# Two transformer blocks on one core: the norms of the second block keep the last chunk in PSUM, and the third unit starts inside the norm

## Chip, core and metric

The kernel runs on one core of a Trainium2 chip. The metric is the device time of one execution in microseconds (us); lower is better. The engines are named as in the profile: PE (TensorE matmul), PEld (its weight loads), DVE (VectorE), ACT (ScalarE), POOL (GpSimd) and SP (SyncE, which issues the loads).

## The reference, cut to what matters

`x` is 512 tokens by 1024 channels. The first block (attention, a state-space branch and a convolutional FFN) runs once and hands `x` on. The second block has two layers, and each layer has three sublayers, each with a norm ahead of it and one behind it:

```python
def _rmsnorm_2(x, g):
    x32 = x.astype(jnp.float32)
    y = x32 * lax.rsqrt(jnp.mean(x32 * x32, axis=-1, keepdims=True) + RMS_EPS)
    return (y * g.astype(jnp.float32)).astype(x.dtype)

def _swiglu(h, w_gate, w_up, w_down):
    return (jax.nn.silu(h @ w_gate) * (h @ w_up)) @ w_down

for l in range(2):
    f = _swiglu(_rmsnorm_2(x, g[0]), ffn_w_gate[l, 0], ffn_w_up[l, 0], ffn_w_down[l, 0])
    x = x + 0.5 * _rmsnorm_2(f, g[1])
    m = _mixer(_rmsnorm_2(x, g[2]), w_in[l], ...)
    x = x + _rmsnorm_2(m, g[3])
    f = _swiglu(_rmsnorm_2(x, g[4]), ffn_w_gate[l, 1], ffn_w_up[l, 1], ffn_w_down[l, 1])
    x = x + 0.5 * _rmsnorm_2(f, g[5])
```

The hidden width of these FFNs is 2816. Where one sublayer ends and the next begins, the kernel needs two token factors: 1/rms of `f` (call it inv_f), with which `x` is updated, and 1/rms of the new `x` (inv_u).

## The kernel before, in words

**Layout.** Channels lie on the 128 partitions, tokens on the free axis. `x`, `f` (output of a sublayer) and `u` (input of the next) are 8 chunks of 128x512. Every float32 product is made of three fp32r products: a weight is split into w_hi (ACT, L1232) and w_lo = raw - w_hi (POOL, L514), an input into u_hi and u_lo. A **unit** is one 128x512 output in a PSUM bank: for each of k chunks three products (lines 655 to 657), so 24 products for 8 chunks and 33 for the 11 chunks of half an FFN's hidden width. Units come in pairs p, slot s=0 into unit_bank0 and s=1 into unit_bank1, and the two weight slots are refilled in turn: SP loads, ACT rounds after the unit before is done, POOL subtracts.

**Order.** Each engine's program is written out by hand, with semaphores between them; there is no planner. An FFN of the second block is done in two halves of the hidden width: 11 pairs of gate and up units, then 4 pairs of down units (`down`, L848) that give the 8 chunks of `f`. After the first half DVE copies the chunks from PSUM into `f` (`f_out`, L2361); in the second half it adds the bank to `f` (`take_f`, L2294). After the mixer it copies them (`take_new`, L2298).

**The norm** (`norm(r)`, r = 1 to 5; r = 0 and r = 6 have code of their own, which the change leaves in essence alone). r = 1, 3, 4 follow an FFN and r = 2, 5 a mixer. While the last four pairs run, DVE and ACT keep running sums over the chunks: squares of f (ACT L1249, DVE L2256), squares of gain times f (ACT L1251, DVE L2231) and x times gain times f (DVE L2235, L2238). From these three sums the mean square of the new `x` follows before the new `x` is there. Then, once the last unit ends:

1. DVE takes the last chunk (L2300 or L2296), ACT squares it (L1249).
2. PE sums over the channels with products against a column of ones (`token_sums`, L710): f_acc at once, the last squares when they come. ACT takes the root (L1242), DVE the reciprocal (L2273), and PE spreads inv_f over a bank (`spread`, L725).
3. DVE meanwhile makes the cross product of the last chunk (L2235, L2238), ahead of the reciprocal, and the last sum of gf_sq (L2231), behind it. PE sums both (16 instructions L710), ACT copies the totals (L1308), and POOL works out the mean square of the new `x` (`grow_x`, L584).
4. DVE updates `x` chunk by chunk (L2351 into a unit bank, L2353), ACT makes u_hi (L1304) and, for six chunks, the unrounded u_all (L1310), POOL the u_lo of those six (L615), DVE the last two (L2285).
5. PE runs `first_units` (L729): the first two units of the next sublayer, side by side, chunk by chunk as `x` comes: four products with u_hi for chunk c (L748), then two with u_lo of chunk c-1 (`low`, L738). Their weights have buffers of their own, and they go into score0 and score1. After chunk 6 inv_u is spread.
6. Then comes the third unit, the first in unit_bank0 (L1200 in an FFN, L917 in the mixer): 24 products. Its bank is one of the two through which DVE updates `x`.

Between the sums PE issues products of the identity with itself, whose result nobody reads (`keep_warm`, L702): 3 after the first sums, 3 after the second, 4 after the last. In the trace each float32 product on PE (sums, spreads, identities) is two instructions.

The mixer's first scores (`z(0)`, L882 to L893) need q and k, which DVE takes after the first two units, turned by four DMAs that SP issues (`turn_heads`, L447 to L456).

## Time and profile before

| what | us |
|---|---|
| median of three runs | 2474.32 (2474.09 to 2474.41) |
| span of the profiled execution | 2472.5 |
| PE busy | 2459.4 (99% of the span) |
| PEld busy | 2010.1 (81%) |
| DVE busy | 1189.9 (48%) |
| POOL busy | 1070.6 (43%) |
| ACT busy | 912.5 (37%) |
| PE's share in the chain that ended last | 85%, with "issue" 9% |

The span runs from the first to the last instruction that the profiler saw, and the device time lies 1.8 us above it. PE's busy time is not PE's best: its matmuls are pipelined, so their recorded durations (390 ns for a 128x512 product) overlap, and the distance from start to start is what a product costs. The five norms r = 1 to 5 begin, with the first sum after the last unit, at 965.15, 1160.99, 1528.77, 1896.58 and 2092.46 us.

### The profile page before, as it was taken

What the parts mean: (1) busy time and instruction counts of PE and PEld (TensorE: products, weight loads), DVE (VectorE), ACT (ScalarE), POOL (GpSimd) and SP (SyncE); (2) the same over time, 40 slices, a digit from 0 to 9 for tenths busy, and PEclk for the clock granted to TensorE, in tenths of its full rate; (3) what the DMA queues carried; (4) which work ended last, traced back from release to release, by engine and by line L of the source; (5) the groups of instructions that cost most, each with busy time, mean ns of one, the idle gap of its engine ahead of it and who ended that gap; (6) DMA issues with size and microseconds to landing.
All of it is one profiled execution on the core that took longest, in us unless ns stands there. A gap on an engine that the chain in (4) does not pass through costs nothing.

```text
span 2472.5 us, 33104 instructions
## 1 busy us (share of the span) xinstructions
PE 2459.4 (99%) x11537; PEld 2010.1 (81%) x11537; DVE 1189.9 (48%) x1736; ACT 912.5 (37%) x1302; POOL 1070.6 (43%) x529
## 2 busy tenths in 40 slices
PE   9999999999999999999999999999999999999999
PEld 6777888888888888778888888888888778888887
DVE  7574866256331345576330345331348666431332
ACT  4444443235322234555331334321234454431332
POOL 5333454444444445334444445444445334443444
PEclk9999999999999999999999999999999999999999
DMA  6222643322233231322232332233231322232232
GB/s 254 86 77 96 229 175 115 114 94 85 85 109 104 93 102 64 98 77 94 85 106 98 101 102 68 85 106 106 93 109 61 91 89 94 77 103 91 95 106 81
DMA packets 74059, 253.42 MB, mean 102 GB/s; under 512 B 9184, under 2 KB 13408, under 8 KB 73856
## 3 DMA queue, kind: packets, MB, share of 16 engines
q1 hardware_dynamic: 73408, 251.93, 30.8%
q8 instruction: 43, 0.70, 0.1%
q10 hardware_dynamic: 576, 0.52, 0.1%
q14 instruction: 32, 0.26, 0.0%
HBM read 244.76 MB, written 2.10 MB: 100 GB/s over the span
## 4 chain that ended last, share of the span: by engine, by line
PE 85%; issue 9%; DVE 3%; POOL 3%; ACT 1%; DMA 0%; SPq 0%; POOLq 0%; DVEq 0%; ACTq 0%
PE unit_bank L655 26%; PE unit_bank L656 26%; PE unit_bank L657 26%; POOL w_lo L514 2%; PE score L748 2%; PE score L738 1%; DVE arena L1732 1%; PE mix L892 1%; PE out_bank L871 1%; PE mix L705 0%; DVE arena L2469 0%; PE out_bank L710 0%; PE mix L971 0%; PE mix L900 0%; DVE arena L2461 0%
## 5 line engine op out<-in xcount | busy, mean ns | idle before, releaser
L514 POOL TENSOR_TENSOR w_lo<-raw,w_hi 128x1024 fp32r<-128x1024 f32 (+2 forms) x374 | 952.6, 2547 | 1299.2 <-ACT w_hi L1232 1299.0
L1232 ACT ACTIVATE w_hi<-raw 128x1024 fp32r<-128x1024 f32 (+2 forms) x375 | 416.6, 1111 | 1170.5 <-PE unit_bank L657 1146.8
L655 PE MATMUL unit_bank<-u_hi,w_hi 128*128 128x512 f32 x2152 | 843.4, 392 | 1.5 <-POOL w_lo L514 1.5
L657 PE MATMUL unit_bank<-u_hi,w_lo 128*128 128x512 f32 x2152 | 837.7, 389 | 0.0
L656 PE MATMUL unit_bank<-u_lo,w_hi 128*128 128x512 f32 x2152 | 837.7, 389 | 0.0
L655 PEld LDWEIGHTS unit_bank<-u_hi,w_hi 128*128 128x128 f32 x2152 | 404.0, 188 | 95.6 <-issue 9.5
L657 PEld LDWEIGHTS unit_bank<-u_hi,w_lo 128*128 128x128 f32 x2152 | 404.0, 188 | 84.7
L656 PEld LDWEIGHTS unit_bank<-u_lo,w_hi 128*128 128x128 f32 x2152 | 404.1, 188 | 82.2 <-issue 0.2
L655 PE MATMUL unit_bank<-h_hi,w_hi 128*128 128x512 f32 x981 | 382.7, 390 | 0.2 <-DVE h_lo L2160 0.2
L657 PE MATMUL unit_bank<-h_hi,w_lo 128*128 128x512 f32 x981 | 381.7, 389 | 0.0
L656 PE MATMUL unit_bank<-h_lo,w_hi 128*128 128x512 f32 x981 | 381.6, 389 | 0.0
L2381 DVE TENSOR_TENSOR arena<-unit_bank,rstd 128x512 f32<-128x512 f32 x84 | 58.1, 691 | 398.9 <-PE unit_bank L657 398.9
L655 PEld LDWEIGHTS unit_bank<-h_hi,w_hi 128*128 128x128 f32 x981 | 184.2, 188 | 39.1 <-DVE h_lo L2160 0.7
L656 PEld LDWEIGHTS unit_bank<-h_lo,w_hi 128*128 128x128 f32 x981 | 184.2, 188 | 38.5 <-issue 0.5
L657 PEld LDWEIGHTS unit_bank<-h_hi,w_lo 128*128 128x128 f32 x981 | 184.2, 188 | 38.4
L2390 DVE TENSOR_TENSOR h_lo<-arena,h_hi 128x512 f32 (+1 forms) x88 | 170.9, 1942 | 78.5 <-ACT h_hi L1601 78.5
L2300 DVE COPY f<-unit_bank 128x512 f32 (+1 forms) x48 | 33.2, 691 | 204.6 <-PE unit_bank L657 203.1
L2378 DVE TENSOR_TENSOR arena<-unit_bank,rstd 128x512 f32<-128x512 f32 x84 | 58.1, 691 | 118.8 <-PE unit_bank L657 118.8
L1601 ACT ACTIVATE h_hi<-arena 128x512 f32 (+1 forms) x88 | 55.6, 632 | 33.9 <-DVE arena L2388 33.4
L2388 DVE TENSOR_TENSOR arena<-arena 128x512 f32<-128x512 f32 x88 | 60.9, 693 | 3.3
L2296 DVE TENSOR_TENSOR f<-unit_bank,f 128x512 f32 (+1 forms) x31 | 21.4, 690 | 75.8 <-PE unit_bank L657 71.5
L1596 ACT ACTIVATE arena<-arena 128x512 f32<-128x512 f32 x88 | 54.0, 614 | 2.7 <-DVE arena L2378 2.7
(399 smaller groups left out, 2073.8 us busy)
## 6 DMA issues: line engine op xcount, KB each, us to landing
raw<-in_w_gate_up SPq DMA_DIRECT2D x168, 512.0 KB, 3.5
raw<-in_w_down SPq DMA_DIRECT2D x64, 704.0 KB, 4.0
raw<-in_w_in SPq DMA_DIRECT2D x65, 512.0 KB, 3.5
raw<-in_w_up SPq DMA_DIRECT2D x30, 512.0 KB, 3.5
f<-in_w_ada_rows SPq DMA_DIRECT2D x26, 512.0 KB, 4.5
raw<-in_w_out SPq DMA_DIRECT2D x24, 512.0 KB, 3.5
raw<-in_w_down SPq DMA_DIRECT2D x16, 512.0 KB, 3.5
ada_in_u<-in_w_ada SPq DMA_DIRECT2D x8, 512.0 KB, 11.1
```

The lines of the kernel that those rows point to most:

```text
L514: e.tensor_tensor(w_lo[:, s, 0:n], raw[:, s, 0:n], as32(w_hi[:, s, 0:n]), ALU.subtract).then_inc(lo_ready, 1)
L655: e.matmul(bank[:], wh, hi(k), start=begin and n == 0, stop=False)
L656: e.matmul(bank[:], wh, lo(k), start=False, stop=False)
L657: mm = e.matmul(bank[:], wl, hi(k), start=False, stop=end and last)
L748: e.matmul(score[s][:], w[:, s, c * P:(c + 1) * P], u_hi[:, c, :], start=c == 0 and w is first_hi, stop=False)
L1232: e.activation(w_hi[:, s, 0:n], raw[:, s, 0:n], ACT.Copy).then_inc(hi_ready, 1)
L1596: e.activation(ffn_s, ffn_g, ACT.Silu).then_inc(silu_ready, 1)
L1601: e.activation(h_hi[:, bass.ds(i, 1), :].rearrange("p a t -> p (a t)"), ffn_h, ACT.Copy).then_inc(hhi_ready, 1)
L2378: g = e.tensor_tensor(ffn_g, banks[0][:], rstd[:], ALU.mult)
L2381: u = e.tensor_tensor(ffn_u, banks[1][:], rstd[:], ALU.mult)
L2388: e.tensor_tensor(ffn_h, ffn_s, ffn_u, ALU.mult).then_inc(hidden_ready, 1)
L2390: e.tensor_tensor(flat(h_lo[:, bass.ds(i, 1), :]), ffn_h, as32(flat(h_hi[:, bass.ds(i, 1), :])), ALU.subtract).then_inc(h_ready, 1)
```

## The change

- The last chunk of `f` is no longer taken out of PSUM by DVE before it is squared. After a mixer it stays in unit_bank1. In the FFNs r = 1, 3, 4 the last down unit of both halves accumulates in one bank (`joined_bank`, mix1): begun in the first half, ended in the second; DVE only increments the semaphore after the first. For this the last pair of `down` stands outside its loop.
- ACT squares that bank as soon as the unit is done; DVE makes the cross product from it when the square is done; after the root ACT squares it with the gain, and copies it into `f`.
- `x` is updated through mix0 and one other bank (`scaled_bank`), so that unit_bank0 is free in the norm. The sums, root_u and the spread of inv_u move to out_bank.
- The third unit's two products with u_hi are issued for chunk 0 and chunk 1 inside `first_units` (`third_high`), after those chunks' other products; `third_rest` does the other 20 after it.
- Identity products of a norm: none after the first sums (3 before), 2 after the second (3 before), none after the last (4 before). They go into score0.

```diff
@@ -216,8 +217,9 @@
         unit_bank, stat_bank, score, mix, out_bank = banks[0:2], banks[2], banks[3:5], banks[5:7], banks[7]
-        square_sum, gf_sum, cross_sum = out_bank[:, 0:TB], mix[0][:, 0:TB], mix[0][:, TB:2 * TB]
-        root_u = mix[0][:, 3 * TB:4 * TB]
+        square_sum, gf_sum, cross_sum = (out_bank[:, n * TB:(n + 1) * TB] for n in (0, 1, 2))
+        root_u = out_bank[:, 3 * TB:4 * TB]
+        first_gf_sum, first_root_u = mix[0][:, 0:TB], mix[0][:, 3 * TB:4 * TB]
         f_run, gf_run, cross_run = score[0][:], score[1][:], mix[0][:]
@@ -228,6 +230,14 @@
         group_bank = (*unit_bank, score[1])
+        joined_bank = mix[1]
+        def last_bank(r):
+            return unit_bank[1] if r % 3 == 2 else joined_bank
+        def scaled_bank(r):
+            return mix[0], (joined_bank if r % 3 == 2 else unit_bank[1])
         consts_loaded = sem("consts_loaded")
@@ -699,7 +710,7 @@
                     mm.then_inc(unit_done, 1)
-            def keep_warm(n, bank=mix[1]):
+            def keep_warm(n, bank=score[0]):
                 for _ in range(n):
@@ -725,6 +736,21 @@
                 mm.then_inc(spread_ready, 1)
+            def third_high(p, c):
+                if c == 0:
+                    e.wait_ge(lo_ready, 2 * p + 1)
+                    e.wait_ge(taken[0], p + 1)
+                for w in (w_hi, w_lo):
+                    e.matmul(unit_bank[0][:], w[:, 0, c * P:(c + 1) * P], u_hi[:, c, :],
+                             start=c == 0 and w is w_hi, stop=False)
+            def third_rest(p, early):
+                for c in range(early):
+                    e.matmul(unit_bank[0][:], w_hi[:, 0, c * P:(c + 1) * P], u_lo[:, c, :], start=False, stop=False)
+                unit(p, 0, from_u, from_u_lo, range(early, DC), first=early, signal="last", begin=False)
             def first_units(q, inserts={}):
@@ -818,20 +844,19 @@
                     token_sums(square_sum, f_acc).then_inc(sums_ready, 1)
-                    token_sums(gf_sum, gf_acc).then_inc(cross_sums, 1)
+                    token_sums(first_gf_sum, gf_acc).then_inc(cross_sums, 1)
                 first_units(FIRST_OF_NORM, {3: sums, 4: lambda: spread(1, inv_f, stat_bank),
                                             6: lambda: spread(2, inv_u, mix[1])})
-            def norm(r):
+            def norm(r, p):
                 e.wait_ge(fsq_added, (DC - 1) * (r + 1))
                 token_sums(square_sum, f_acc, last=False)
-                keep_warm(3)
                 e.wait_ge(fsq_ready, 2 * DC * r + 2 * (DC - 1) + 1)
                 token_sums(square_sum, f_sq, first=False).then_inc(sums_ready, 1)
-                keep_warm(3)
+                keep_warm(2)
                 spread(2 * r + 1, inv_f, stat_bank)
@@ -839,17 +864,23 @@
                 mm.then_inc(cross_sums, 1)
-                keep_warm(4)
-                first_units(FIRST_OF_NORM + r, {6: lambda: spread(2 * r + 2, inv_u, mix[1])})
+                first_units(FIRST_OF_NORM + r, {0: lambda: third_high(p, 0), 1: lambda: third_high(p, 1),
+                                                6: lambda: spread(2 * r + 2, inv_u, out_bank)})
+                third_rest(p, THIRD_EARLY)
             def h_chunk(h0):
                 return lambda c: e.wait_ge(h_ready, h0 + c + 1)
-            def down(p0, h0, n_k, pairs=DC // 2):
-                with e.Fori(0, pairs) as i:
+            def down(p0, h0, n_k, pairs=DC // 2, joined=None):
+                looped = pairs if joined is None else pairs - 1
+                with e.Fori(0, looped) as i:
                     unit(p0 + i, 0, from_h, from_h_lo, range(n_k), before=h_chunk(h0))
                     unit(p0 + i, 1, from_h, from_h_lo, range(n_k))
+                if joined is not None:
+                    p = p0 + looped
+                    unit(p, 0, from_h, from_h_lo, range(n_k))
+                    unit(p, 1, from_h, from_h_lo, range(n_k), bank=joined_bank, begin=joined == 0, end=joined == 1)
             def turn_v(free, free_at, src_sem, src_at, done):
@@ -1197,20 +1227,22 @@
                         if half == 0:
-                            unit(p0 + 1, 0, from_u, from_u_lo, EIGHT)
+                            if l == 0 and s_ffn == 0:
+                                unit(p0 + 1, 0, from_u, from_u_lo, EIGHT)
                             in_unit(p0 + 1, 1)
...
                         last = r == NORMS - 1 and half == 1
-                        down(p0 + HALF2, 16 + 44 * l + 22 * s_ffn + HALF2 * half, HALF2, DC // 2 - last)
+                        down(p0 + HALF2, 16 + 44 * l + 22 * s_ffn + HALF2 * half, HALF2, DC // 2 - last,
+                             half if r < NORMS - 1 else None)
                     if last:
...
                     else:
-                        norm(r)
+                        norm(r, (ffn2(l + 1, 0) if s_ffn else mix2(l)) + 1)
                     if s_ffn == 0:
@@ -1295,9 +1327,14 @@
                     return
-                f_squares(p, 1, part, DC - 1, g)
+                e.wait_ge(unit_done, 2 * p + 2)
+                e.wait_ge(fsq_added, (DC - 1) * (r + 1))
+                e.activation(f_sq, last_bank(r)[:], ACT.Square).then_inc(fsq_ready, 1)
                 e.wait_ge(sums_ready, r + 1)
                 token_root(root_f, square_sum)
+                e.wait_ge(taken[1], p + 2)
+                e.activation(gf_sq, last_bank(r)[:], ACT.Square, scale=g(DC - 1)).then_inc(fsq_ready, 1)
+                e.activation(f[:, DC - 1, :], last_bank(r)[:], ACT.Copy).then_inc(last_kept, 1)
                 for c in range(DC):
@@ -1305,7 +1342,7 @@
                         n = 2 * TB if r else TB
-                        e.activation(totals[:, 0:n], mix[0][:, 0:n], ACT.Copy).then_inc(totals_ready, 1)
+                        e.activation(totals[:, 0:n], out_bank[:, TB:TB + n], ACT.Copy).then_inc(totals_ready, 1)
                     if c < DC - 2:
@@ -1313,7 +1350,7 @@
                 e.wait_ge(spread_ready, 2 * r + 2)
-                e.activation(rstd[:], mix[1][:], ACT.Copy).then_inc(rstd_ready, 1)
+                e.activation(rstd[:], out_bank[:], ACT.Copy).then_inc(rstd_ready, 1)
             def first_norm(p):
@@ -2240,8 +2277,14 @@
                 def chunk(p, s, c, ahead_of_last=0):
+                    if ahead_of_last == 1:
+                        e.wait_ge(fsq_ready, 2 * (DC * r + c) + 1)
+                        cross_of(c, last_bank(r)[:])
+                        e.sem_inc(taken[s], 1)
+                        add_cross(cross_acc)
+                        return
                     e.wait_ge(unit_done, 2 * p + s + 1)
-                    direct = crossed and take is take_new and ahead_of_last != 1
+                    direct = crossed and take is take_new
                     if direct:
@@ -2249,9 +2292,7 @@
                     if crossed:
-                        add_cross(cross_acc if ahead_of_last == 1 else cross_run)
-                    if ahead_of_last == 1:
-                        return
+                        add_cross(cross_run)
                     e.wait_ge(fsq_ready, 2 * DC * r + (2 if ahead else 1) * c + 1)
@@ -2346,11 +2387,13 @@
                 return lambda c: table[:, bass.ds(at + (2 * r - 1) * DC + c, 1)]
-            def post_norm(g):
+            def post_norm(r, g):
                 def update(c):
-                    step(e.scalar_tensor_tensor(unit_bank[c % 2][:], f[:, c, :], g(c), stat_bank[:], ALU.mult,
-                                                ALU.mult))
-                    e.tensor_tensor(x[:, c, :], unit_bank[c % 2][:], x[:, c, :], ALU.add).then_inc(x_ready, 1)
+                    out = scaled_bank(r)[c % 2][:]
+                    if c == DC - 1:
+                        e.wait_ge(last_kept, r)
+                    step(e.scalar_tensor_tensor(out, f[:, c, :], g(c), stat_bank[:], ALU.mult, ALU.mult))
+                    e.tensor_tensor(x[:, c, :], out, x[:, c, :], ALU.add).then_inc(x_ready, 1)
                 return update
@@ -2358,12 +2401,18 @@
             for l in range(LAYERS):
-                def f_out(p0):
-                    with e.Fori(0, DC // 2) as i:
+                def f_out(p0, joined):
+                    with e.Fori(0, DC // 2 - joined) as i:
                         for s in range(2):
...
                             take_new(p0 + i, s, 2 * i + s)
+                    if joined:
+                        p = p0 + DC // 2 - 1
+                        e.wait_ge(unit_done, 2 * p + 1)
+                        take_new(p, 0, DC - 2)
+                        e.wait_ge(unit_done, 2 * p + 2)
+                        e.sem_inc(taken[1], 1)
                 for s_ffn in range(2):
```

## Rows read from the trace of the kernel before

**Rows 1.** Windows: two stretches, every engine; (x) counts instructions, PEclk the granted clock.
```profile
core 0: us, PE busy (x) PEld busy (x) DVE busy (x) ACT busy (x) POOL busy (x), PEclk, DMA share, GB/s
1160.98:1180.60 19.62, 19.39 (x117) 16.59 (x116) 15.29 (x24) 13.69 (x22) 10.62 (x12) 1.00 0.07 25
...
1180.61:1528.76 348.15, 348.15 (x1537) 288.38 (x1536) 122.03 (x134) 102.67 (x119) 156.89 (x60) 1.00 0.30 100
```

**Rows 2.** Timeline of PE in the norm r=2 (start us, us, what).
```profile
1160.99 0.95 PE L710 MATMUL out_bank<-tabs,arena 128*128 128x1 f32 x8
...
1162.60 1.05 PE L710 MATMUL out_bank<-tabs,arena 128*128 128x1 f32 x8
...
1164.29 1.16 PE L725 MATMUL stat_bank<-tabs,arena 128*128 128x128 f32 x8
1165.28 1.84 PE L710 MATMUL mix<-tabs,arena 128*128 128x1 f32 x16
1166.99 1.14 PE L705 MATMUL mix<-tabs 128*128 128x128 f32 x8
1167.88 0.71 PE L748 MATMUL score<-u_hi,first_hi 128*128 128x512 f32 x2
...
1170.47 0.73 PE L738 MATMUL score<-u_lo,first_hi 128*128 128x512 f32 x2
...
1180.61 0.39 PE L655 MATMUL unit_bank<-u_hi,w_hi 128*128 128x512 f32 x1
```

**Rows 3.** Timeline of DVE in the norm r=2.
```profile
1161.19 0.69 DVE L2300 COPY f<-unit_bank 128x512 f32<-128x512 f32 x1 [1.77 <-PE unit_bank L657]
1161.92 0.75 DVE L2235 SCALAR_TENSOR_TENSOR arena<-x,cols,f 128x512 f32<-128x512 f32 x1
1162.70 0.69 DVE L2238 TENSOR_TENSOR arena<-mix,arena 128x512 f32<-128x512 f32 x1
1164.06 0.18 DVE L2273 RECIPROCAL arena<-arena 128x4 f32<-128x4 f32 x1 [0.66 <-ACT arena L1242]
1164.15 0.66 DVE L2231 TENSOR_TENSOR arena<-score,arena 128x512 f32<-128x512 f32 x1
1165.48 0.75 DVE L2351 SCALAR_TENSOR_TENSOR unit_bank<-f,cols,stat_bank 128x512 f32<-128x512 f32 x1 [0.67 <-PE stat_bank L725]
1166.27 0.69 DVE L2353 TENSOR_TENSOR x<-unit_bank,x 128x512 f32<-128x512 f32 x1
```

**Rows 4.** Timeline of ACT in the norm r=2.
```profile
1161.92 0.63 ACT L1249 ACTIVATE arena<-f 128x512 f32<-128x512 f32 x1 [3.41 <-DVE f L2300]
1162.45 0.71 ACT L1251 ACTIVATE arena<-f,cols 128x512 f32<-128x512 f32 x1
1163.69 0.26 ACT L1242 ACTIVATE arena<-out_bank,eps 128x4 f32<-128x4 f32 x1 [0.53 <-PE out_bank L710]
1167.00 0.72 ACT L1304 ACTIVATE u_hi<-x,cols 128x512 fp32r<-128x512 f32 x1 [3.04 <-DVE x L2353]
1167.62 0.16 ACT L1308 ACTIVATE arena<-mix 128x8 f32<-128x8 f32 x1
```

**Rows 5.** Timeline of POOL in the norm r=2.
```profile
1156.89 2.41 POOL L514 TENSOR_TENSOR w_lo<-raw,w_hi 128x1024 fp32r<-128x1024 f32 x1
...
1169.12 7.61 POOL L615 TENSOR_TENSOR u_lo<-arena,u_hi 128x512 fp32r<-128x512 f32 x6
```

**Rows 6.** Timeline of SP's queue after the norm r=1.
```profile
986.51 2.48 SPq L456 DMA_DIRECT2D us<-arena  x4
```

**Rows 7.** Source view of L456: the landing times of its transfers.
```profile
DMA to landing us min/median/max: 2.2/2.3/2.4
```

**Rows 8.** Timeline of PE, the first scores of the mixer after r=1.
```profile
993.02 0.69 PE L892 MATMUL mix<-us 64*128 64x512 f32 x1
```

**Rows 9.** Windows of the instructions of L971, at the start of the program.
```profile
3.90:9.50 5.60, 5.54 (x7) 2.44 (x8) 1.00 0.94 350
9.60:13.20 3.60, 3.60 (x9) 1.52 (x8) 1.00 1.04 389
```

More of the change, by code:

```diff
@@ L76 @@
 CONV_STEPS = 2
+THIRD_EARLY = 2
 WIDEST_FIRST = (3, 2, 1, 0)
@@ L310, in program @@
         f_scaled, x_summed = sem("f_scaled"), sem("x_summed")
+        last_kept = sem("last_kept")
         def col(name, i=0, n=1):
@@ L915, in head_pair @@
                     turn_logs(1)
-                unit(pm + 1, 0, from_u, from_u_lo, EIGHT)
                 e.wait_ge(first_taken, 2 * (FIRST_OF_NORM + 3 * l + 1) + 2)
@@ L935, in mixer2 @@
                     unit(pm + MIX2_IN + i, 1, from_h, from_h_lo, EIGHT)
-                norm(3 * l + 2)
+                norm(3 * l + 2, ffn2(l, 1) + 1)
             def ada_part(half, k):
@@ L1350, in first_norm @@
                 e.wait_ge(cross_sums, 1)
-                e.activation(totals[:, 0:TB], gf_sum, ACT.Copy).then_inc(totals_ready, 1)
+                e.activation(totals[:, 0:TB], first_gf_sum, ACT.Copy).then_inc(totals_ready, 1)
                 e.wait_ge(grown_ready, 1)
-                token_root(root_u, x_sum)
+                token_root(first_root_u, x_sum)
                 refill(p + 1, 1)
@@ L2339, in first_norm @@
                         e.wait_ge(root_ready, 2)
-                        step(e.reciprocal(inv_u, root_u))
+                        step(e.reciprocal(inv_u, first_root_u))
                         e.tensor_tensor(inv_u, inv_u, inv_f, ALU.mult).then_inc(inverse_ready, 1)
@@ L2397, in _ @@
                         if half == 0:
-                            f_out(p0 + HALF2)
-                    norm(r, p0 + HALF2, take_f, f, post_gain(r), post_norm(post_gain(r)))
+                            f_out(p0 + HALF2, r < NORMS - 1)
+                    norm(r, p0 + HALF2, take_f, f, post_gain(r), post_norm(r, post_gain(r)))
                     if s_ffn:
@@ L2545, in _ @@
                                                as32(h_hi[:, 6 + m, :]), ALU.mult, ALU.subtract).then_inc(cat_ready, 1)
-                    norm(r, pm + MIX2_IN, take_new, f, post_gain(r), post_norm(post_gain(r)))
+                    norm(r, pm + MIX2_IN, take_new, f, post_gain(r), post_norm(r, post_gain(r)))
 def _tiles(w):
```

## The prediction

> **What bounds the kernel now.** I read the page first: PE is busy 99% of the span, so only PE's time counts, and the question is where PE does something other than products of units. The windows answer it. In the FFN stretch after the norm r=2, PE issues 1536 unit products in 348.15 us [rows 1], which is 0.2267 us for each and leaves no gap: nothing that happens on another engine there can show. The stretch of the norm itself is 19.62 us [rows 1], with 48 products of first_units in it (10.88 us at that pitch) and one spread. It occurs five times (r = 1 to 5) with the same count of PE instructions, 117, and the same length to 0.03 us, so I work out one and multiply by five. The granted clock is 1.00 in it.
>
> PE's timeline of the norm [rows 2] shows three parts. From the first sum (1160.99) to the first product with u_hi (1167.88) are 6.89 us of sums, spreads and identity products, that is, waiting. From there to the first product with u_lo (1170.47) are 2.59 us, in which only 8 products run (1.81 us). From 1170.47 to the first product of the third unit (1180.61) are 10.14 us, with 40 products (9.07 us) and the spread of inv_u (0.8 us): that part is full, and ends when PE is done, whatever x does. So the norm ends later or sooner by when u_lo of chunk 0 comes, and by how many products stand behind that point.
>
> u_lo of chunk 0 is POOL's, which starts at 1169.12 [rows 5]. Followed back through the timelines of ACT and DVE: totals copied at 1167.62 behind u_hi at 1167.00 [rows 4], x updated at 1166.27, scaled at 1165.48, reciprocal at 1164.06 [rows 3], root at 1163.69 [rows 4], sums at 1162.60 [rows 2], square at 1161.92 [rows 4], and DVE's copy out of the bank at 1161.19 [rows 3]. This chain is what the change shortens.
>
> **Head of the norm.** Two branches meet at the reciprocal.
> - Root: ACT can square when DVE could copy, at 1161.19 instead of 1161.92, 0.73 us sooner. How long a Square from PSUM takes here no row shows; I take the 0.63 us of the one from SBUF [rows 4], with 0.60 to 0.75 as bounds (0.75 is DVE's product from SBUF, the slowest of this size). It ends at 1161.82, PE's sums of f_acc (issued over 0.8 us from 1160.99) are just over, the sums follow 0.05 later as they do now, and the root, 1.09 after the sums, runs from 1162.96 to 1163.22.
> - Cross product: DVE must now wait for the square. It reacts to ACT in 0.11 (root ends 1163.95, reciprocal 1164.06) and so starts at 1161.93, by chance where it starts today (1161.92). It then takes 0.78 + 0.69 [rows 3] and ends at 1163.40. The reciprocal stands behind it on DVE, and starts at 1163.44.
>
> The second branch ends last, so the reciprocal comes at 1163.44 and not at 1163.33: a gain of 0.62, not of the 0.73 of the copy. Bounds: 0.50 if the square takes 0.75, and 0.73 if DVE reacts at once.
>
> What stands behind the new steps: on ACT, gf_sq (0.71) moves behind the root, to 1163.15 to 1163.9, and a copy of 0.6 to 0.7 is new, ending by 1164.6. ACT is next wanted for u_hi, at 1166.38, so both cost nothing; without that cover they would cost their 1.3 us. DVE's last add of gf_sq starts at 1164.0 instead of 1164.15 and ends at 1164.7; the spread of inv_f reaches DVE 1.42 after the reciprocal, at 1164.86, so the add is covered, by 0.2 us only. PE's 16 instructions of sums follow at about 1164.8 and are over by 1166.6, and ACT wants them at 1167.00: covered by 0.4. DVE's semaphore increments are bounded by nothing and 0.1 each, and taken as covered. DVE's copy in the first half of three FFNs goes; PE hides it [rows 1], so nothing. The update through mix0 instead of unit_bank0 has the same operations: nothing. The last down pair outside its loop, six times: the mixer's code stands outside loops too, and a loop's 1536 products show no turn, so nothing. The joined bank changes no count on PE.
>
> So everything from the reciprocal to u_lo of chunk 0 shifts by **0.62 us**.
>
> **Third unit.** Four of its 24 products move into the norm. The two of chunk 0 and the four of each of chunks 0 and 1 must fit ahead of the first product with u_lo: 10 x 0.227 = 2.27 us, and 2.59 are there. So the first two cost nothing. The two of chunk 1 stand behind that product, in the full part, and cost what they save. Gain: 2 x 0.227 = **0.45 us**, with bounds of 0 (PE's waits take as long as before) and 0.72 (if u_lo of chunk 0 came early enough to take in all four, less 0.2). What they wait for, w_lo of the slot, is there at 1159.30 [rows 5]. After the norm of r = 1 and 4 the scores wait for DMAs: SP issues them from 986.51 to 988.99 [rows 6], they land within 2.4 us [rows 7], by 991.4, and PE wants them at 993.02 [rows 8]. The first two units end only 0.2 sooner, PE gets there 1.07 sooner, at 991.95; against 991.2, still covered.
>
> **Identity products.** After the first sums none is needed for time. The last four end at about the time u_hi comes [rows 2]; at most 0.1 us of delay goes with them, in front of the first product and not of the u_lo that decides: nothing. Two rather than three before the spread: it starts 0.05 after the reciprocal's end either way.
>
> **Sum.** 5 x (0.62 + 0.45) = 5.35 us. The profiled span of 2472.5 would be 2467.1; the median lies 1.8 above the span, and 2474.32 - 5.35 gives **2468.9**. The bounds give 5 x 0.50 = 2.5 to 5 x 1.45 = 7.3.
>
> **The clock.** The granted clock is 1.00 in the norm [rows 1], with 10 identity products in each; the change leaves 2, and a wait of some 0.6 us without any work ahead of the first u_hi. The Trainium skill ("TensorE: Matmul & The Clock Gate", Part 1) says that the array's clock is halved unless recent activity holds it up, which speaks against this change; the trace shows no fall in any norm, so it neither bears this out nor excludes it with fewer products.
>
> **Rivals.**
> 1. *The head does not shorten.* The waits of one reader of the bank for the other take the place of the copy: the cover of 0.2 us over DVE's gf add is thin, and ACT does root, gf_sq and copy in a row. Were half of the 0.62 lost, 5 x (0.31 + 0.45) = 3.8 us are left: 2470.5. For it: the two branches at the reciprocal are within 0.11. Against it: each link is one the trace shows. 12%.
> 2. *The early products only move the wait.* PE comes to u_lo later by what it has just issued; then only 5 x 0.62 = 3.1 stay: 2471.2. Against it: 2.27 fits in 2.59. 8%.
> 3. *The clock falls in the norm* (slower). No row shows a clock under 1.00, but at the start of the program the same product of L971 runs 7 times in 5.60 us and then 9 times in 3.60 [rows 9]: 0.80 against 0.40, PE at half pace for at least 5.6 us. As much in a norm costs 2.8 us, against 1.07 gained: 5 x 1.73 = 8.6 slower, 2482.9. Two norms of the five decide it (5.6 lost). For it: idle and one-column sums fill more of the head. Against it: 6.89 us of hardly any products, five times, left the clock at 1.00, and the head becomes shorter. 8%.
> 4. *It does not do what it says*: PE waits elsewhere, for instance at the mixer's scores, where 0.8 us of cover are left, and nothing is gained: 2474.3. 2%.
>
> **Numbers.** My forecast has 70%. A difference of 0.2%, 4.95 us, is about what a measurement can tell from no change; the forecast lies 0.4 us beyond it, so its small misses count as the same: of the 70, 57 faster and 13 the same. Rivals 1 and 2 give the same (20), or, where they take only little, faster (2 of them); the clock gives slower (8), and 2 stay the same. Together 0.59 faster, 0.33 the same, 0.08 slower. The range goes from 2467.0 (1.45 in every norm) to 2472.0 (rivals 1 and 2 with 0.8 to spare); the slower cases are left out.
>
> **What would show it.** Distance from the first sum to the first product with u_hi: 6.2 to 6.3 us instead of 6.89; ACT's square at the time at which DVE copied; the reciprocal 2.45 after the first sum instead of 3.07; from the first u_lo product to the end of the first units 10.6 instead of 10.14, then 20 products; PEclk 1.00 in all norms; 117 less 16 identity instructions plus 4. I am wrong if the reciprocal waits for something other than the cross product, if the first product with u_lo comes more than 2.7 after the first with u_hi, or if a norm shows a clock below 1.

## The result

The changed kernel takes 2478.71 us (median of 21 runs, 2471.11 to 2481.85) against 2473.82 (21 runs, 2473.19 to 2475.22) for the kernel before. The ratio is 1.0013 with an interval of 1.0007 to 1.0019: slower, by 0.13% (the medians alone differ by 0.20%), where 0.22% faster was forecast, and outside the stated range. By the prediction's own measure of 0.2% that is no more than what can just be told from no change. The scatter is news too: it was 2 us and is now 11. Each run lists its mean granted clock, and the time follows it: 0.998 in the runs of 2471.1 and 2471.8, 0.994 at 2477.2 to 2478.7, 0.992 at 2481.3 and 2481.9. The profiled execution took 2479.72 with a span of 2477.9.

The page of the changed kernel, four of its parts: span, PE's busy time, the granted clock in tenths, and the chain that ended last.

```profile
span 2477.9 us, 32896 instructions
...
PE 2463.6 (99%) x11457; PEld 2015.2 (81%) x11457; DVE 1174.1 (47%) x1728; ACT 913.3 (37%) x1307; POOL 1071.8 (43%) x529
...
PEclk9999999999999999999999999999999999999999
...
PE 84%; issue 9%; DVE 4%; POOL 2%; ACT 1%; DMA 0%; SPq 0%; POOLq 0%; DVEq 0%; ACTq 0%
```

PE's busy share is the same as before, and the row of the clock shows nine everywhere, since a slice there is 62 us long. The windows show what it hides. These are the five norms, each from its first sum, 19.62 us long like [rows 1]; PEclk is the granted clock.

```profile
core 0: us, PE busy (x) PEld busy (x) DVE busy (x) ACT busy (x) POOL busy (x), PEclk, DMA share, GB/s
964.02:983.64 19.62, 19.38 (x86) 16.83 (x85) 15.51 (x23) 12.04 (x21) 10.61 (x12) 0.74 0.00 0
1162.38:1182.00 19.62, 19.39 (x86) 16.95 (x85) 15.52 (x23) 12.04 (x21) 10.28 (x12) 0.74 0.06 25
1532.71:1552.33 19.62, 18.58 (x106) 15.86 (x105) 14.82 (x24) 14.28 (x23) 10.93 (x12) 1.00 0.00 1
1899.43:1919.05 19.62, 19.39 (x86) 16.89 (x85) 15.51 (x23) 12.04 (x21) 10.47 (x12) 0.74 0.00 1
2097.85:2117.47 19.62, 18.71 (x101) 16.14 (x100) 14.70 (x23) 13.19 (x23) 10.92 (x12) 0.91 0.07 26
```

In the kernel before, every one of these stretches had 1.00 and 117 PE instructions. Now r = 1, 2 and 4 have 0.74, r = 5 has 0.91, and only r = 3 keeps 1.00. The trace's record of the granted clock, from which the column is worked out, holds four falls to 0.5 in the span, which are 1.2 GHz instead of 2.4 (a window laid over the first of them alone, 967.12 to 977.36, has 0.50): at 967.1, 1165.1 and 1902.4 us for 10.24 us each, and at 2103.8 for 3.41. They come 3.1, 2.7, 3.0 and 5.9 us after the first sum of their norms.

The norm r = 3 had no fall, and shows the change as it was meant. PE's timeline of it answers to [rows 2]:

```profile
1532.71 1.90 PE L721 MATMUL out_bank<-tabs,arena 128*128 128x1 f32 x16
1534.48 0.69 PE L716 MATMUL score<-tabs 128*128 128x128 f32 x4
1535.40 1.16 PE L736 MATMUL stat_bank<-tabs,arena 128*128 128x128 f32 x8 [0.23 <-DVE arena L2314]
1536.40 1.88 PE L721 MATMUL out_bank<-tabs,arena 128*128 128x1 f32 x16
1538.98 0.70 PE L774 MATMUL score<-u_hi,first_hi 128*128 128x512 f32 x2 [0.70 <-ACT u_hi L1341]
1539.52 0.62 PE L774 MATMUL score<-u_hi,first_lo 128*128 128x512 f32 x2
1539.97 0.39 PE L746 MATMUL unit_bank<-u_hi,w_hi 128*128 128x512 f32 x1
1540.20 0.39 PE L746 MATMUL unit_bank<-u_hi,w_lo 128*128 128x512 f32 x1
...
1541.60 0.73 PE L764 MATMUL score<-u_lo,first_hi 128*128 128x512 f32 x2
1542.17 0.39 PE L746 MATMUL unit_bank<-u_hi,w_hi 128*128 128x512 f32 x1
1542.40 0.40 PE L746 MATMUL unit_bank<-u_hi,w_lo 128*128 128x512 f32 x1
...
1552.17 0.62 PE L752 MATMUL unit_bank<-u_lo,w_hi 128*128 128x512 f32 x2
```

ACT's timeline of the same norm answers to [rows 4]:

```profile
1532.91 0.60 ACT L1332 ACTIVATE arena<-mix 128x512 f32<-128x512 f32 x1 [5.29 <-PE mix L668]
1534.65 0.26 ACT L1274 ACTIVATE arena<-out_bank,eps 128x4 f32<-128x4 f32 x1 [1.14 <-PE out_bank L721]
1534.82 0.68 ACT L1336 ACTIVATE arena<-mix,half_g 128x512 f32<-128x512 f32 x1
1535.39 0.60 ACT L1337 ACTIVATE f<-mix 128x512 f32<-128x512 f32 x1
1538.11 0.72 ACT L1341 ACTIVATE u_hi<-x,cols 128x512 fp32r<-128x512 f32 x1 [2.13 <-DVE x L2396]
```

DVE's answers to [rows 3]:

```profile
1533.54 0.75 DVE L2272 SCALAR_TENSOR_TENSOR arena<-x,half_g,mix 128x512 f32<-128x512 f32 x1 [4.44 <-ACT arena L1332]
1534.44 0.69 DVE L2275 TENSOR_TENSOR arena<-mix,arena 128x512 f32<-128x512 f32 x1 [0.15 <-DVE arena L2272]
1535.17 0.18 DVE L2314 RECIPROCAL arena<-arena 128x4 f32<-128x4 f32 x1
1535.53 0.69 DVE L2268 TENSOR_TENSOR arena<-score,arena 128x512 f32<-128x512 f32 x1 [0.18 <-ACT arena L1336]
1536.60 0.75 DVE L2395 SCALAR_TENSOR_TENSOR mix<-f,half_g,stat_bank 128x512 f32<-128x512 f32 x1 [0.38 <-PE stat_bank L736]
```

ACT squares the bank 0.20 after the first sum, where it squared the copy 0.93 after it [rows 2, 4]. The second sums no longer have a row of their own, since they follow the first without a wait (x16). The reciprocal comes at 2.46 (1535.17 - 1532.71) instead of 3.07, the first product with u_hi at 6.27 instead of 6.89, the first with u_lo at 8.89 instead of 9.48. The products L746 are the third unit's: four of them run before 1542.63, and at 1552.17, 19.46 after the first sum, 20 are left. Before, 24 were left at 19.62 (19.65 in this norm). So this norm gained 0.19 + 4 x 0.227 = 1.1 us.

The norm r = 2 of the same execution fell 2.7 us after its first sum (PE's timeline, from the identity products to the first product with u_hi):

```profile
1164.14 0.69 PE L716 MATMUL score<-tabs 128*128 128x128 f32 x4
1165.07 2.08 PE L736 MATMUL stat_bank<-tabs,arena 128*128 128x128 f32 x8 [0.23 <-DVE arena L2314]
1166.94 3.41 PE L721 MATMUL out_bank<-tabs,arena 128*128 128x1 f32 x16
1170.21 1.20 PE L774 MATMUL score<-u_hi,first_hi 128*128 128x512 f32 x2
```

The 16 instructions of sums take 3.41 instead of 1.88 us, and two products of 512 columns 1.20 instead of 0.70. The third unit's rest begins 23.08 us after the first sum, not 19.46: 3.6 us lost. The falls of r = 1 and 4 cost as much (23.06 and 23.05), the short one of r = 5 1.1 (20.54). Gained are 5 x 1.1 = 5.5, lost 3 x 3.6 + 1.1 = 11.9: 6.4 net. The spans differ by 5.4, because in the profiled execution of before two products at 297.5 us stand 1.70 us apart, and the same two 0.50 in this one, so that before's first norm begins 1.1 us later; in all kernels run, of either order, that norm begins between 963.95 and 965.15 us.

### The profile page after: what moved, and what is told of

It is laid out like the page before. It is cut to its first block, busy times and chain, and to the rows that moved or that the text cites. A ratio compares the mean times of both kernels' runs of the same rounds, so it can differ in the third digit from the quotient of the medians.

```text
span 2477.9 us, 32896 instructions
## 1 busy us (share of the span) xinstructions
PE 2463.6 (99%) x11457; PEld 2015.2 (81%) x11457; DVE 1174.1 (47%) x1728; ACT 913.3 (37%) x1307; POOL 1071.8 (43%) x529
## 4 chain that ended last, share of the span: by engine, by line
PE 84%; issue 9%; DVE 4%; POOL 2%; ACT 1%; DMA 0%; SPq 0%; POOLq 0%; DVEq 0%; ACTq 0%
PE unit_bank L666 25%; PE unit_bank L667 25%; PE unit_bank L668 25%; PE score L774 2%; POOL w_lo L525 2%; PE score L764 1%; DVE arena L1769 1%; PE mix L668 1%; PE mix L667 1%; PE mix L666 1%; PE mix L923 1%; PE out_bank L902 1%; PE out_bank L721 0%; DVE arena L2518 0%; PE mix L931 0%
## 5 line engine op out<-in xcount | busy, mean ns | idle before, releaser
L666 PE MATMUL unit_bank<-h_hi,w_hi 128*128 128x512 f32 x915 | 357.0, 390 | 0.2 <-DVE h_lo L2197 0.2
L668 PE MATMUL unit_bank<-h_hi,w_lo 128*128 128x512 f32 x915 | 356.0, 389 | 0.0
L667 PE MATMUL unit_bank<-h_lo,w_hi 128*128 128x512 f32 x915 | 355.9, 389 | 0.0
L666 PEld LDWEIGHTS unit_bank<-h_hi,w_hi 128*128 128x128 f32 x915 | 171.8, 188 | 36.6 <-DVE h_lo L2197 0.6
L667 PEld LDWEIGHTS unit_bank<-h_lo,w_hi 128*128 128x128 f32 x915 | 171.8, 188 | 35.9 <-issue 0.5
L668 PEld LDWEIGHTS unit_bank<-h_hi,w_lo 128*128 128x128 f32 x915 | 171.8, 188 | 35.8
```

What stands on the lines that cost most here:

```text
L666: e.matmul(bank[:], wh, hi(k), start=begin and n == 0, stop=False)
L667: e.matmul(bank[:], wh, lo(k), start=False, stop=False)
L668: mm = e.matmul(bank[:], wl, hi(k), start=False, stop=end and last)
```

## The experiments

The identity products of a norm are given as three numbers: behind the first sums, behind the second, behind the last. Before they were 3, 3, 4; in the change 0, 2, 0. The first four kernels separate two causes of the falls: the identity products that went, or the order and waits of the change itself. The kernel before was measured beside each series: 2473.55 us for the first four, 2473.62 for `ident_0_4_0`, `third_late`, `only_third_early` and `early_before_low`, 2473.73 for `before_ident_0_4_3`; each ratio is to the one of its own series.

**All identity products back in the changed kernel** (`ident_all_back`):

```diff
                 token_sums(square_sum, f_acc, last=False)
+                keep_warm(3)
...
-                keep_warm(2)
+                keep_warm(3)
                 spread(2 * r + 1, inv_f, stat_bank)
...
                 mm.then_inc(cross_sums, 1)
+                keep_warm(4)
                 first_units(...)
```

> The changed kernel with all identity products of the norms put back (3, 3 and 4). Theory (the clock falls because the identity products are gone): the granted clock is 1.00 in all five norms and the runs stop scattering. The three products after the first sums now stand in front of the sums of the last squares, which are ready 0.85 us after the first sum: they delay them by some 0.7 us, so the reciprocal comes at about 3.06 again and the head gains nothing; the third unit still gives 0.45. So 5 x 0.45 = 2.2 us under the kernel before. Rival (the change's own waits let the clock fall, whatever the identities): falls in several norms as in the changed kernel, and a time above the kernel before.

Measured: 2471.43 us (2470.21 to 2475.34), ratio 0.9993 (0.9984 to 1.0002), not told from the kernel before. The reciprocal is at 2.92, 0.15 sooner, a little more than expected. The first product with u_hi gains nothing by it (6.92 after the first sum, r = 2, against 6.89), since it stands behind the four identity products, though ACT begins u_hi 0.15 sooner (5.86 after the first sum against 6.01): 3.78 us lie between the start of the spread and that product, against 3.59 before. The falls at 3 us are gone, but the profiled execution has two, of 3.41 us, 6.6 after the first sum (r = 1 and r = 5), each costing 1.4, where the profiled execution of the kernel before, with the same counts, had none. The runs still scatter over 5 us, which the theory did not expect. So the theory holds for most of it, and the rival has a share.

**As many as fit: 0, 4, 3** (`ident_0_4_3`):

```diff
-                keep_warm(2)
+                keep_warm(4)
                 spread(2 * r + 1, inv_f, stat_bank)
...
                 mm.then_inc(cross_sums, 1)
+                keep_warm(3)
                 first_units(...)
```

> The changed kernel with 0, 4 and 3 identity products: as many as fit into PE's waits behind the second and the last sums without delaying anything. Theory (identities hold the clock): fewer falls than in the changed kernel or none; with none, 5.4 us under the kernel before (2468.4 against 2473.8), with every fall adding up to 3.6 us. Rival (change's own waits): as the changed kernel, 3 us above the kernel before in the mean and 10 us of scatter.

Measured: 2467.95 us (2467.76 to 2468.85), ratio 0.9977 (0.9968 to 0.9986). The windows of its five norms (columns as above):

```profile
964.97:984.59 19.62, 19.55 (x116) 16.95 (x115) 14.71 (x23) 14.26 (x23) 10.95 (x12) 1.00 0.00 1
1159.79:1179.41 19.62, 19.54 (x116) 16.95 (x115) 14.80 (x24) 14.26 (x23) 10.93 (x12) 1.00 0.06 22
1526.52:1546.14 19.62, 19.52 (x116) 16.93 (x115) 14.81 (x24) 14.27 (x23) 10.93 (x12) 1.00 0.00 1
1893.25:1912.87 19.62, 19.55 (x116) 16.95 (x115) 14.71 (x23) 14.26 (x23) 10.94 (x12) 1.00 0.00 1
2088.11:2107.73 19.62, 19.53 (x116) 16.97 (x115) 14.85 (x24) 14.30 (x23) 10.93 (x12) 1.00 0.06 24
```

PEclk is 1.00 in all five, the first u_hi comes at 6.25 to 6.27 in each, and the third unit's rest begins at 19.44 to 19.48. The change with seven identity products is 5.6 us faster than the kernel before; with two it is slower. The theory is borne out.

**Only the last four: 0, 2, 4** (`ident_0_2_4`): the edit is the `keep_warm(4)` of the first experiment alone.

> The changed kernel with only the four identity products behind the last sums put back (0, 2, 4). In the changed kernel three of the four falls come 2.7 to 3.1 us after the norm's first sum, before these four would run. Theory that the first half of the head decides: falls stay at about 3 us after the first sum, the late one (5.9) goes; about 2 us above the kernel before. Rival that the last four decide: no falls, 5.4 us under the kernel before.

Measured: 2475.44 us (2472.80 to 2484.10), ratio 1.0011 (1.0003 to 1.0020). The falls stand at 3.1, 3.6 and 2.7 us after the first sum (r = 1, 3, 4), and none late. Here the two falls of 10.24 us cost 4.5 each and not 3.6 (the third unit's rest at 23.98 and 23.94 instead of 19.46): the four identity products in front of the first u_hi run at half the clock as well. What runs behind the last sums comes too late to hold the clock in the first part of the head.

**The kernel before with 0, 2, 0** (`before_ident_0_2_0`):

```diff
                 token_sums(square_sum, f_acc, last=False)
-                keep_warm(3)
...
-                keep_warm(3)
+                keep_warm(2)
                 spread(2 * r + 1, inv_f, stat_bank)
...
-                keep_warm(4)
                 first_units(...)
```

> The kernel before with nothing changed but the identity products of the norms: 0, 2 and 0 instead of 3, 3 and 4. Theory (identities hold the clock): falls as in the changed kernel, with none of its gains: each costs up to 3.6 us, about four of five norms: 8 to 14 us slower than the kernel before. Rival (the change's own waits let the clock fall): granted clock 1.00 throughout and the time of the kernel before within 0.5 us.

Measured: 2481.42 us (2479.80 to 2483.78), ratio 1.0030 (1.0018 to 1.0041), 7.9 us over the kernel before in the medians. Its norms:

```profile
964.29:983.91 19.62, 18.01 (x96) 15.22 (x95) 15.29 (x24) 12.55 (x21) 10.59 (x12) 0.91 0.00 0
1161.30:1180.92 19.62, 18.18 (x90) 15.68 (x89) 15.29 (x24) 12.06 (x20) 9.42 (x12) 0.83 0.06 21
1531.35:1550.97 19.62, 18.88 (x95) 16.43 (x94) 16.09 (x24) 11.77 (x21) 10.53 (x12) 0.83 0.00 1
1900.64:1920.26 19.62, 18.88 (x84) 16.22 (x83) 16.09 (x24) 11.62 (x20) 9.93 (x12) 0.74 0.00 1
2099.72:2119.34 19.62, 18.39 (x90) 15.84 (x89) 15.29 (x24) 12.06 (x20) 9.61 (x12) 0.83 0.06 23
```

All five have falls, two of them twice. Taking away identity products alone, with nothing else of the change, costs about as much as the theory said, just under its range.

**0, 4, 0 in the changed kernel** (`ident_0_4_0`): `keep_warm(4)` behind the second sums, nothing behind the last.

> The changed kernel with 0, 4 and 0 identity products: it takes from the 0-4-3 kernel the three behind the last sums. Theory (each group holds the clock against a fall in its own part of the head): the falls at about 3 us after the first sum stay away, those at 5 to 7 us come in one or two norms of five; 2469 to 2473, with scatter. Rival (the second group alone is enough): 2468.0 and no fall in a norm.

Measured: 2472.17 us (2470.64 to 2474.03), ratio 0.9994 (0.9985 to 1.0003). No fall at 3 us; four norms of five fall for 3.41 us, at 6.5, 7.0, 7.7 and 6.2 after the first sum, each costing 1.2 (the rest of the third unit at 20.64 to 20.70). These are more norms than expected, the last of them later than expected, and the time is in the expected range. The three behind the last sums are worth 4.2 us (2472.17 - 2467.95).

**0, 4, 3 in the kernel before** (`before_ident_0_4_3`), with its DVE copy ahead of the square:

```diff
                 token_sums(square_sum, f_acc, last=False)
-                keep_warm(3)
...
-                keep_warm(3)
+                keep_warm(4)
...
-                keep_warm(4)
+                keep_warm(3)
                 first_units(...)
```

> The kernel before with 0, 4 and 3 identity products. The four behind the second sums take 0.9 us and push the spread 0.1 or less; else nothing of its course changes, but the wait of 0.8 us between the first and the second sums is now without work. Theory (what counts is the work in each part of the head, and the changed kernel can do without the first group because it has no wait there): falls at 2 to 4 us after the first sum in some norms, 1 to 3.6 us each; 2475 to 2481 with scatter. Rival (0, 4, 3 is simply enough): the time of the kernel before within 0.5 us, no falls.

Measured: 2483.30 us (2480.26 to 2484.96), ratio 1.0035 (1.0023 to 1.0048), above the expected range. PE's timeline of its norm r = 5, from the first sums to the last:

```profile
2097.62 0.95 PE L710 MATMUL out_bank<-tabs,arena 128*128 128x1 f32 x8
2099.22 1.05 PE L710 MATMUL out_bank<-tabs,arena 128*128 128x1 f32 x8 [0.66 <-ACT arena L1248]
2100.14 1.14 PE L705 MATMUL mix<-tabs 128*128 128x128 f32 x8
2101.11 1.53 PE L725 MATMUL stat_bank<-tabs,arena 128*128 128x128 f32 x8
2102.44 3.41 PE L710 MATMUL mix<-tabs,arena 128*128 128x1 f32 x16
```

Between the first sums and the second stands a wait of 0.66 us, which the changed kernel does not have, since ACT squares sooner. The fall comes 3.9 us after the first sum; those of r = 1 and r = 3 come at 3.8 and 2.7. The same counts that hold the clock in the changed kernel do not hold it here, and seven identity products do no better in this order than the two of `before_ident_0_2_0` (2481.42 us): the first group can be left out only together with the copy.

The next three measure the two terms of the sum and look for more, in kernels whose norms show no fall in the profile.

**The third unit late again** (`third_late`), on top of 0, 4, 3:

```diff
-                first_units(FIRST_OF_NORM + r, {0: lambda: third_high(p, 0), 1: lambda: third_high(p, 1),
-                                                6: lambda: spread(2 * r + 2, inv_u, out_bank)})
-                third_rest(p, THIRD_EARLY)
+                first_units(FIRST_OF_NORM + r, {6: lambda: spread(2 * r + 2, inv_u, out_bank)})
+                unit(p, 0, from_u, from_u_lo, EIGHT)
```

> The changed kernel with 0, 4 and 3 identity products, and the third unit begun after the first two, as before the change. It measures the term of 0.45 us per norm: theory 5 x 0.45 = 2.3 us over the 0-4-3 kernel, 2470.2, and 3.1 under the kernel before, which is the head's share alone. Rival (the early products only moved a wait): within 0.3 us of the 0-4-3 kernel. Fewer products in the wait ahead of u_lo: if a fall of the clock shows it would be 1 us or more above this in single runs.

Measured: 2470.41 us (2470.13 to 2471.88), ratio 0.9986 (0.9977 to 0.9995). That is 2.46 us over the 0-4-3 kernel, 0.49 per norm against 0.45 in the sum. In the traces it is 0.43: at 19.00 us after the first sum 24 products of the third unit are left, against 20 at 19.47 in the 0-4-3 kernel. No norm fell.

**Only the third unit early** (`only_third_early`), with 3, 3, 4 and the last chunk handled as before:

```diff
-                e.wait_ge(unit_done, 2 * p + 2)
+                e.wait_ge(taken[1], p + 2)
                 e.wait_ge(fsq_added, (DC - 1) * (r + 1))
-                e.activation(f_sq, last_bank(r)[:], ACT.Square).then_inc(fsq_ready, 1)
+                e.activation(f_sq, f[:, DC - 1, :], ACT.Square).then_inc(fsq_ready, 1)
+                e.activation(gf_sq, f[:, DC - 1, :], ACT.Square, scale=g(DC - 1)).then_inc(fsq_ready, 1)
                 e.wait_ge(sums_ready, r + 1)
                 token_root(root_f, square_sum)
-                e.wait_ge(taken[1], p + 2)
-                e.activation(gf_sq, last_bank(r)[:], ACT.Square, scale=g(DC - 1)).then_inc(fsq_ready, 1)
-                e.activation(f[:, DC - 1, :], last_bank(r)[:], ACT.Copy).then_inc(last_kept, 1)
...
-                        e.wait_ge(fsq_ready, 2 * (DC * r + c) + 1)
-                        cross_of(c, last_bank(r)[:])
-                        e.sem_inc(taken[s], 1)
+                        e.wait_ge(unit_done, 2 * p + s + 1)
+                        e.tensor_copy(row(f, c), last_bank(r)[:]).then_inc(taken[s], 1)
+                        e.wait_ge(taken[s], p + 2)
+                        cross_of(c, row(f, c))
                         add_cross(cross_acc)
...
                     out = scaled_bank(r)[c % 2][:]
-                    if c == DC - 1:
-                        e.wait_ge(last_kept, r)
```

> The changed kernel with the handling of the last chunk undone: DVE copies it out of PSUM first, ACT squares the copy, twice, ahead of the root, and the identity products are 3, 3 and 4, as in the kernel before. What is left of the change is the third unit's early start (and the joined bank). Theory: the reciprocal at 3.06 us after the first sum, the first u_hi at 6.89, no falls as in the kernel before, and 5 x 0.45 = 2.3 us under it: 2471.3. Rival (the third unit's early start or the joined bank costs the clock): falls at 6 to 7 us after the first sum in some norms, as seen with all identity products back.

Measured: 2471.36 us (2471.05 to 2472.47), ratio 0.9990 (0.9981 to 0.9999), 2.26 us under the kernel before in the medians. DVE's timeline of its norm r = 2, whose first sum is at 1160.31:

```profile
1160.51 0.69 DVE L2282 COPY f<-unit_bank 128x512 f32<-128x512 f32 x1 [1.77 <-PE unit_bank L668]
1161.24 0.75 DVE L2272 SCALAR_TENSOR_TENSOR arena<-x,cols,f 128x512 f32<-128x512 f32 x1
1162.03 0.69 DVE L2275 TENSOR_TENSOR arena<-mix,arena 128x512 f32<-128x512 f32 x1
1163.38 0.18 DVE L2315 RECIPROCAL arena<-arena 128x4 f32<-128x4 f32 x1 [0.66 <-ACT arena L1276]
```

Copy, cross product and its sum stand where they stood, and the reciprocal is at 3.07 again; the first u_hi is at 6.89 in all norms and no norm fell. So neither the early products nor the joined bank touch the clock here, and the falls with all identity products back point to the other order of the head. The mean clocks of the runs say the same: ten of 11 runs list 1.00 here, five of 11 in `ident_all_back`. What in that head lets the clock go at 6.6 us was not taken further apart.

**Chunk 1's early products ahead of the first u_lo** (`early_before_low`), on top of 0, 4, 3:

```diff
+                    if c == 1 and q > FIRST_OF_NORM:
+                        inserts[1]()
                     if c:
                         low(c - 1)
-                    if c in inserts:
+                    if c in inserts and (c != 1 or q <= FIRST_OF_NORM):
                         inserts[c]()
```

> The changed kernel with 0, 4 and 3 identity products (2467.95 in the first series) and the third unit's two products with u_hi of chunk 1 issued ahead of the first product with u_lo instead of behind it. Theory (from the first u_lo product on PE is full, and ahead of it there is a wait): 12 products of 0.227 stand between the first u_hi and the first u_lo product, which is then issued 2.8 instead of 2.62 us after, and 0.45 of work is gone behind it: 0.25 less per norm, 1.3 us in all, 2466.7. Rival (the wait only moves): the same time within 0.3. Clock 1.00 in all norms.

Measured: 2466.34 us (2465.99 to 2467.62), ratio 0.9970 (0.9959 to 0.9981), 1.6 us under the 0-4-3 kernel. PE's timeline of its norm r = 2 around the first product with u_lo (L764):

```profile
1165.54 0.70 PE L774 MATMUL score<-u_hi,first_hi 128*128 128x512 f32 x2
...
1167.92 0.39 PE L746 MATMUL unit_bank<-u_hi,w_hi 128*128 128x512 f32 x1
1168.15 0.39 PE L746 MATMUL unit_bank<-u_hi,w_lo 128*128 128x512 f32 x1
1168.37 0.62 PE L764 MATMUL score<-u_lo,first_hi 128*128 128x512 f32 x2
```

It comes 2.83 us after the first with u_hi (1168.37 - 1165.54), at the pitch of PE and without a wait, as expected. The gain is larger than the 1.3 us expected: in the traces the third unit's rest begins at 19.09 to 19.12 instead of 19.44 to 19.48, 0.36 less per norm and not 0.25. One part of it is in the rows: two products with u_lo take 0.62 us here, and 0.73 where a wait stands ahead of them (at 1541.60 above). This is the fastest kernel of the study: 7.3 us under the kernel before.

## Why the prediction was wrong

Its working of the norm was right, and it failed at the clock, which it had as a rival. Of its own signs of being wrong the last came true: four norms of five show a clock below 1.

- **Head.** The reciprocal was put 0.62 us sooner, behind the cross product and not behind the root. In r = 3 it comes at 2.46 instead of 3.07, right behind the cross sum (1534.44 + 0.69), with the root ended at 1534.91 before it. That it came out to 0.01 us was luck in part, since sizes inside were off and cancelled: the Square from PSUM took 0.60 and not 0.63, DVE started 0.03 after its end and not 0.11, and its second step stood 0.15 behind the first and not 0.03. The sums, gf_sq and the copy stayed covered, as said: the add of gf_sq ends at 1536.22 and the update starts at 1536.60.
- **Third unit.** 0.45 per norm was said, 0.49 measured (third_late; 0.43 in its trace), 0.45 (only_third_early).
- **Sum.** 5.35 us was the forecast of what both give; the 0-4-3 kernel, which is not the change that was forecast, shows 5.6, at 2467.95, inside the range given, with a clock of 1.00 in the norms.
- **The step that failed** is the item on the identity products: "After the first sums none is needed for time", the last four "nothing", the third before the spread no difference "either way". Each group was priced by the time that it takes or frees on PE, and at nothing. They did their work elsewhere, in the clock. Eight of ten gone cost 7.9 us in the kernel before (before_ident_0_2_0), and the changed kernel with seven of them (0-4-3) stands 10.8 us under the one with two in the medians (2478.71 - 2467.95; the kernel before of the two series differs by 0.3).
- **Rival 3** had the mechanism, the place and the sign, and was given 8%. Its argument against itself was that 6.89 us of hardly any products left the clock at 1.00. That read the identity products as hardly any: ten of them, 20 instructions of 0.11 us, were 2.2 of the 6.89 us of PE's issue, and the change takes 1.8 of these away. Its price, 2.8 us for a fall, was the half of a slow stretch of 5.6 us; a fall lasts 3.41, 6.83 or 10.24 us here and costs 1.1 (r = 5 of the change) to 4.5 (ident_0_2_4). Its "Two norms of the five decide it" holds for falls as long as those of the change (2 x 3.6 = 7.2 against 5.5 gained); in the profiled execution four norms fell.
- **The Trainium skill** ("TensorE: Matmul & The Clock Gate", Part 1: the array's clock is halved unless recent activity holds it up) spoke against the change, and the trace now agrees, with 0.74 for PEclk in three norms. It was weighed by the fact that no fall showed before, but the products that prevented it were what the change took away.
- Rivals 1, 2 and 4 did not happen: the head shortened by its full 0.6, the early products went into a wait (1.30 us between the first u_hi products of chunks 0 and 1 in third_late, of which four products fill 0.9), and the mixer's scores were not held up (in the 0-4-3 kernel they begin at 991.80, 0.32 after the last product ahead of them, as before the change).

## What to carry to other kernels

An instruction whose result nobody reads may still save more time than it takes: before one is removed from a wait of PE, ask what else PE does in that stretch, and take a clock of 1.00 in the trace as a statement about the kernel with the instruction, not without it. Make such a change in two steps, the shortening of the path and the removal of filler, since the first can gain what the second loses. A wait that is filled with real products of the next unit, as far as they are ready, is worth more than one filled with identities: here it gave 0.45 us per norm, and 0.8 where both pairs of early products stood in the wait.

## What was not expected of the hardware

The same program took 2471.1 to 2481.9 us, and the time follows the mean clock of the run. A profile shows the falls of one execution only; that the other runs differ by how many of their norms fell and for how long is concluded from that mean. Over all profiles the early falls stand 2.3 to 4.3 us after the first sum, the late ones 5.9 to 9.3. Each lasted 3.41, 6.83 or 10.24 us, apart from those at the end of the program. A fall also showed outside the norms, at 335.1 us in the 0-4-3 kernel and at 335.6 in `early_before_low`, in the spread and the identity products ahead of the first block's FFN, a stretch of which the change alters only the bank that the identity products write; it lasted 3.41 us both times. The kernel before is not free of falls either: its profile shows none ahead of the end, but 23 of the 69 runs beside the experiments list a mean clock of 0.999, and these take 2473.96 us or more. Where they fell is not on record, so the absence of falls in its norms is shown for the profiled execution and not for every run. Three identity products (0.7 us of PE's waiting time) moved the median by 4.2 us.
